# Two-layer hybrid decoder: sums of squares of the keys and the copies of two sets of transposes moved to ScalarE, three PSUM banks in turn, gating a tile later

## The chip, the cores and the metric

The program runs on one core of a Trainium2 chip. A core has TensorE (matrix multiplication, written PE in the profile, its weight loads PEld), VectorE (DVE), ScalarE (ACT), GpSimd (POOL) and SyncE (SP, which issues most DMAs). Each engine runs its own instruction stream in order and waits on semaphores for the others. The metric is the device time of one execution in microseconds (us); less is better.

## The reference

Two layers, each a mixer and a feed-forward part, for 512 new tokens (the prompt) and 8 tokens of a decode batch that share the weights. The mixer has one input projection whose columns go to a gated DeltaNet (group A, 4 heads of 128) and to a retention (group B, 4 heads of 128). What the change touches:

```python
qkv = silu(causal_conv(p_qkv, conv_w))                 # group A: q, k, v
qa, ka = l2norm(heads(q)), l2norm(heads(k))            # x * rsqrt(sum(x*x) + 1e-6), per token and head
a_low  = strict_lower((k*beta) @ k^T * decay)          # per chunk and head
u      = solve(I + a_low, v * beta)                    # v rows scaled by beta, one number per token and head
...
o_b = retention(rope(q_b), rope(k_b), v_b)             # group B
o_b = o_b * rsqrt(mean(o_b*o_b) + EPS) * ret_norm_w * silu(gate_b)
out = concat([o_a, o_b]) @ w_out
```

## The kernel before

Activations are kept transposed (features on the 128 partitions, tokens along the free axis). A weight tile of the input projection is 1024 x 128; the loop counter `t` runs over its 32 tiles of a layer: 0 to 11 retention q, k and v; 12 to 15 keys of group A; 16 to 19 the retention's gate (`gatesB`); 20 to 23 values of group A; 24 to 27 queries of group A; 28 to 31 gate of group A. Every matrix product is made of three fp32r passes: each weight tile (a slab) comes by DMA into `stage` (SP), ScalarE rounds it to `Wh` (line 1064), VectorE makes the rest `Wl` (line 1435), and `mm6` multiplies Xh·Wh, Xl·Wh, Xh·Wl for two halves of 260 columns. A tile has 8 steps of 6 such matmuls (`proj(1)` is one step, line 626). The result lies in one of two pairs of PSUM banks (0 to 3), so tile t can start only when VectorE has read tile t-2 (`tile_free0/1`).

Between the steps of the projection TensorE does the smaller work of both mixers, in an order that is written out by hand (lines 817 to 960), in banks 4 to 7. All four engines have such hand-written streams: what a `if t == 17:` holds is issued after tile 17's own work of that engine. The pieces of the change:

- `stats(i, c)`, line 718: sums of squares of a key or query head for one of 4 chunks of 128 tokens, as a matmul of the squares `sqb` with a column of ones. ScalarE makes the squares at the end of `silu_tile` (line 1180). Keys have i = 0 to 3, queries 4 to 7; each takes 4 matmuls. The keys' are put between the steps of tiles 15, 16 and 17.
- `k_rows(c)`, line 706: transposes of the keys of chunk c into PSUM; `k_copy(c)`, line 1182: ScalarE copies them to `ktok`.
- `prep(c)`, line 729: the decay exponents of chunk c (bank 5) and k·k^T (bank 6). ScalarE turns the first into `PT` by Exp with the log of the keys' root as bias (`decays`, line 1186), VectorE masks it and multiplies (`masked`, line 1555, gives `MT` and `mt_ready`), TensorE transposes (`blocks_T`), VectorE scales (`blocks_scaled`, gives `Ab` and `a_ready`). `Ab` goes by DMA to DRAM and back for a solve by VectorE (`solve`, tiles 21 to 23).
- `ret_normed(c)`, line 1612: VectorE scales the retention's rows `oR` by their roots.
- `ret_out(c)`, line 755: TensorE transposes these rows into bank 5 or 6, after tile 24, half of 25, 25, and half of 26. `gate_ret(c)`, line 1580: VectorE multiplies bank, norm weight and `gatesB`.
- `v_rows(c)`, line 694, and `v_scaled(c)`, line 1543: the value rows, transposed by TensorE, scaled by beta into `bv` by VectorE.
- `left(i)` and `right(i)`, lines 766 and 780: TensorE's steps of a block inverse that follow, beginning in tile 28.

## Time and profile before

| what | value |
|---|---|
| median of 3 runs | 1521.31 us (1519.15 to 1521.94) |
| profiled execution | 1518.86 us, its span 1517.1 us |
| PE busy | 1480.3 us, 98% of the span |
| DVE, ACT, POOL busy | 844.0, 507.2, 104.5 us |
| chain that ended last | PE 86%, DVE 8%, ACT 2%, DMA 2% |
| granted TensorE clock | 0.998 |

The span goes from the first to the last instruction of the profiled execution; the run's own time is 1.8 us more. A fp32 matmul of the program shows as two rows of instructions, a fp32r one as one row. Layer 0 lasts from 0 to about 750 us of the span, layer 1 from there; what is read in one layer at time x is found in the other at about x + 747.

### The profile page before, as it was taken

To read this page: it belongs to the slowest core of one execution; us is meant where nothing else is said; L and a number is where in the kernel's file an instruction comes from. 1 tells how busy PE (TensorE), PEld (TensorE's weight loads), DVE (VectorE), ACT (ScalarE), POOL (GpSimd) and SP (SyncE) were. 2 spreads that over 40 slices of the span, in tenths; PEclk is the share of its full clock that TensorE was granted. 3 is DMA by queue.
4 is the path that set the end of the run, shared out by engine and by line. 5 is a ranking of instruction groups with operands and counts; after the bars stand their busy time and mean duration, and the time that the engine had idled before them with its cause. 6 is when DMAs were issued, how large, how long until landed. Compare 5 with 4: busy or idle time off the path is not lost.

```text
span 1517.1 us, 28272 instructions
## 1 busy us (share of the span) xinstructions
PE 1480.3 (98%) x12164; PEld 1463.0 (96%) x12164; DVE 844.0 (56%) x1438; ACT 507.2 (33%) x919; POOL 104.5 (7%) x145
## 2 busy tenths in 40 slices
PE   7999999999999999999999999999999999999996
PEld 6999999999999999999989999999999999999996
DVE  3745685478555554423396457845785555543235
ACT  4124432435422222222241344424363222222221
POOL 0000012210000000000000001121000000000000
PEclk9999999999999999999999999999999999999999
DMA  4232133022233434222213222321223334332221
GB/s 163 98 112 84 56 102 102 29 70 76 98 126 128 144 127 145 88 95 95 73 62 106 98 84 63 101 71 39 76 71 119 132 130 142 128 116 89 93 98 57
DMA packets 57403, 147.38 MB, mean 97 GB/s; under 512 B 19008, under 2 KB 22464, under 8 KB 57280
## 3 DMA queue, kind: packets, MB, share of 16 engines
q1 hardware_dynamic: 49456, 119.88, 24.2%
q0 software_dynamic: 7824, 25.70, 4.8%
q8 instruction: 96, 1.57, 0.4%
q14 instruction: 27, 0.22, 0.1%
HBM read 132.77 MB, written 12.78 MB: 96 GB/s over the span
## 4 chain that ended last, share of the span: by engine, by line
PE 86%; DVE 8%; ACT 2%; DMA 2%; issue 1%; SPq 1%; DVEq 0%; ACTq 0%
PE PS L525 69%; PE PS L531 5%; DVE Wl L1435 2%; PE PS L544 2%; DMA stage<-w_slabs 1%; PE PS L690 1%; DVE upd L1469 1%; DVE hT L1470 1%; DVE conv L1537 1%; ACT Wh L1064 1%; PE PS L777 1%; PE PS L792 1%; PE PS L794 1%; PE PS L725 1%; DVE Xl L1452 1%
## 5 line engine op out<-in xcount | busy, mean ns | idle before, releaser
L525 PE MATMUL PS<-Xh,Wh 128*128 128x260 f32 x2464 | 514.4, 290 | 13.4 <-DVE Wl L1435 11.1
L525 PE MATMUL PS<-Xh,Wl 128*128 128x260 f32 x2464 | 496.8, 283 | 0.0
L525 PE MATMUL PS<-Xl,Wh 128*128 128x260 f32 x2464 | 496.2, 283 | 0.0
L1064 ACT ACTIVATE Wh<-stage 128x1024 fp32r<-128x1024 f32 x212 | 224.6, 1060 | 725.3 <-PE PS L525 711.8
L525 PEld LDWEIGHTS PS<-Xh,Wh 128*128 128x128 f32 x2464 | 382.9, 189 | 17.2 <-DVE Wl L1435 11.5
L525 PEld LDWEIGHTS PS<-Xl,Wh 128*128 128x128 f32 x2464 | 381.2, 189 | 0.0
L525 PEld LDWEIGHTS PS<-Xh,Wl 128*128 128x128 f32 x2464 | 380.2, 189 | 0.0
L1435 DVE TENSOR_TENSOR Wl<-stage,Wh 128x1024 fp32r<-128x1024 f32 x212 | 259.2, 1223 | 191.6 <-ACT Wh L1064 191.3
L525 PE MATMUL PS<-actH,Wh 128*128 128x260 f32 x616 | 124.4, 283 | 0.0
L525 PE MATMUL PS<-actH,Wl 128*128 128x260 f32 x616 | 123.9, 282 | 0.0
L525 PE MATMUL PS<-actL,Wh 128*128 128x260 f32 x616 | 123.8, 282 | 0.0
L1920 DVE TENSOR_TENSOR up<-PS,rb 128x520 f32<-128x520 f32 x44 | 30.8, 699 | 142.3 <-PE PS L525 142.3
L525 PEld LDWEIGHTS PS<-actL,Wh 128*128 128x128 f32 x616 | 95.1, 188 | 0.0
L525 PEld LDWEIGHTS PS<-actH,Wh 128*128 128x128 f32 x616 | 94.8, 188 | 0.0
L525 PEld LDWEIGHTS PS<-actH,Wl 128*128 128x128 f32 x616 | 94.8, 188 | 0.0
L531 PE MATMUL PS<-Xh,Wh 128*128 128x260 f32 x224 | 74.0, 330 | 0.5 <-DVE Wl L1435 0.4
L1909 DVE TENSOR_TENSOR gp<-PS,rb 128x520 f32<-128x520 f32 x44 | 30.8, 699 | 63.9 <-PE PS L525 58.3
L531 PE MATMUL PS<-Xl,Wh 128*128 128x260 f32 x224 | 63.3, 283 | 0.0
L531 PE MATMUL PS<-Xh,Wl 128*128 128x260 f32 x224 | 63.3, 282 | 0.0
L1537 DVE SCALAR_TENSOR_TENSOR conv<-raw,prm,conv 128x544 f32<-128x544 f32 x72 | 57.1, 793 | 2.4 <-ACT conv L1164 0.5
L435 POOL DMA_DIRECT2D dst<-state_ret x32 | 17.3, 542 | 457.4 <-DVE rcs L1500 294.9
L531 PEld LDWEIGHTS PS<-Xh,Wh 128*128 128x128 f32 x224 | 42.3, 189 | 2.7 <-DVE Wl L1435 0.6
(287 smaller groups left out, 1718.3 us busy)
## 6 DMA issues: line engine op xcount, KB each, us to landing
stage<-w_slabs SPq DMA_DIRECT2D x212, 512.0 KB, 3.3
dst<-state_ret POOLq DMA_DIRECT2D x32, 256.0 KB, 3.0
dst<-state_gdn POOLq DMA_DIRECT2D x32, 256.0 KB, 3.0
out_gdn_sample<-dst POOLq DMA_DIRECT2D x16, 256.0 KB, 2.8
out_ret_sample<-dst POOLq DMA_DIRECT2D x16, 256.0 KB, 3.2
hT<-x_t SPq DMA_DIRECT2D x4, 520.0 KB, 6.8
out_y_t<-hT SPq DMA_DIRECT2D x2, 520.0 KB, 3.0
out_y_t<-hT SPq DMA_DIRECT2D x2, 390.0 KB, 2.6
```

Source lines behind the costliest of these rows:

```text
L435: pool.dma_start(dst[:, u % 2], src).then_inc(s[f"dst{u % 2}_loaded"], 16)
L525: ins = mm(PS[:, 2 * slot + a, 0:HC], w[:, ws, pos, :], x[:, a, :], start=first and w is Wh and x is xh, stop=last and w is Wl)
L531: ins = mm(PS[:, 2 * slot + a, 0:HC], w[:, ws, pos, :], x[:, a, :], start=first and w is Wh and x is xh, stop=last and w is Wl)
L544: mm(PS[:, 4 + a, 0:HC], ones, sqh[:, k % 2, a, :], start=k == 0, stop=k == KT - 1).then_inc(s["x_sums"], 1)
L690: ins = mm(PS[:, 7, at_:at_ + 2], dst[:, u % 2, i, :], qkvD[:, h:2 * H + h + 1:2 * H, b], start=True, stop=True)
L725: ins = mm(PS[:, 7, at_:at_ + 1], sqb[:, i % 2, c * P:(c + 1) * P], ones[:, 0:1], start=True, stop=True)
L777: ins = mm(PS[:, 4, j * P:(j + 1) * P], T[:, i % 2, j, :], firsts(2 * (i % 2) + j // 2, b, j % 2), start=True, stop=True)
L1064: A(Wh[:, G % NW], stage[:, G % NS], ACT.Copy).then_inc(s["hi_split"], 1)
L1435: V.tensor_tensor(Wl[:, G % NW], stage[:, G % NS], Wh[:, G % NW].bitcast(fp32), ALU.subtract).then_inc(s["lo_split"], 1)
L1537: ins = V.scalar_tensor_tensor(conv[:, u], raw[:, u, w:w + CONV_N], prm[:, l, row + w * QKV:row + w * QKV + 1], conv[:, u], ALU.mult, ALU.add)
L1909: freed(V.tensor_tensor(gp[:], pj(3 if j == 1 else 0), rb[:], ALU.mult), t)
L1920: freed(V.tensor_tensor(up[:], pj(1), rb[:], ALU.mult), t + 1)
```

## The change

- The keys' 16 `stats` matmuls of a layer are gone, with the 4 squares that fed them. ScalarE instead takes the sums from the transposed rows `ktok`: 16 activations (Square, with the sum of a row as second output), 3 of 4 chunks before tile 17's weight rounding, the last after it. The root is then one Ln, one scale by -0.5, and one Exp, the Exp behind `decays(0)`.
- Without the stats between them, TensorE reaches `k_rows(0..2)` half a tile earlier in the program (middle of tile 17), `k_rows(3)` too; `prep(0)` stays at the middle of tile 18.
- On VectorE in tile 17 `masked(0)` and `decay_sums(2)` come ahead of the small products with the keys' root. The normalising of the retention rows (4 `ret_normed`) moves from tile 17 to the end of tile 19.
- The retention's transposes use banks 5, 6, 4, 5. ScalarE copies each out of PSUM with the norm weight as scale into `bv`, which is free then (`ret_out_rows`); `gate_ret` becomes a product of two SBUF tiles and comes a tile later. TensorE's next user of a bank waits for the copy (`rO_ready`) in place of the gating (`catR_done`).
- The value rows use banks 6, 4, 5, 6, and ScalarE scales them into `bv`, 4 activations a chunk (`v_scaled`), in place of one VectorE product.
- Waits of `left(0)` and `right(0)` are split to match.

TensorE, end of tile 17's steps and the keys' transposes, before (L525 is a projection step, L725 stats, L715 k_rows):

```order
L525 MATMUL PS<-Xh,Wl 128x260 x2
L725 MATMUL PS<-cf,sqb 128x1
L525 MATMUL PS<-Xh,Wh 128x260 x2
L525 MATMUL PS<-Xl,Wh 128x260 x2
L525 MATMUL PS<-Xh,Wl 128x260 x2
L725 MATMUL PS<-cf,sqb 128x1
L715 MATMUL PS<-cf,kT 128x128 [waits oR_ready,rs_ready,silu_done]
L715 MATMUL PS<-cf,kT 128x128 x11
L525 MATMUL PS<-Xh,Wh 128x260 [waits tile_free0,lo_split]
```

and now, at the middle of tile 17 (L526 is the projection step, L714 k_rows):

```order
L526 MATMUL PS<-Xh,Wh 128x260 x2
L526 MATMUL PS<-Xl,Wh 128x260 x2
L526 MATMUL PS<-Xh,Wl 128x260 x2
L714 MATMUL PS<-cf,kT 128x128 [waits oR_ready,rs_ready,silu_done]
L714 MATMUL PS<-cf,kT 128x128 x11
L526 MATMUL PS<-Xh,Wh 128x260 x2
```

The one-column matmuls are gone, and the transposes are followed by the rest of tile 17 (no wait for a free pair of banks there) where they were followed by tile 18.

ScalarE, from the last key tile to the first decays, before (L1180 squares, L1064 weight rounding, L1184 k_copy, L1189 decays):

```order
L1174 ACTIVATE qkvD<-conv 128x8
L1180 ACTIVATE sqb<-kT 128x512 [waits st_mm,silu_done]
L1064 ACTIVATE Wh<-stage 128x1024 [waits tile_done,slab0_loaded]
L1054 ACT_TABLE_LOAD
L1238 ACTIVATE nrR<-nrR 128x16 [waits nrR_pre]
L1239 ACTIVATE nrR<-nrR 128x16 [waits act_step]
L1242 ACTIVATE lrq<-PS 128x4x4 [waits st_mm]
L1243 ACTIVATE rq<-lrq 128x4x4 [waits act_step]
L1244 ACTIVATE lrq<-lrq 128x4x4 [waits act_step]
L1184 ACTIVATE ktok<-PS 128x512 [waits k_T] x4
L1189 ACTIVATE PT<-PS,lrq 128x128 [waits dec_mm,kst_ready]
L1189 ACTIVATE PT<-PS,lrq 128x128 x3
```

and now (L1188 the sums, L1061 weight rounding, L1181 k_copy, L1194 decays; ahead of these rows stand the table load, three k_copy and the sums of two chunks):

```order
L1188 ACTIVATE sqb,lrq<-ktok 128x128 [waits kt_ready]
L1188 ACTIVATE sqb,lrq<-ktok 128x128 x3
L1181 ACTIVATE ktok<-PS 128x512 [waits k_T]
L1061 ACTIVATE Wh<-stage 128x1024 [waits tile_done,slab0_loaded]
L1188 ACTIVATE dump,lrq<-ktok 128x128 [waits kt_ready]
L1188 ACTIVATE dump,lrq<-ktok 128x128 x3
L1261 ACTIVATE lrq<-lrq 128x4x4 [waits ksq_ready]
L1262 ACTIVATE lrq<-lrq 128x4x4 [waits act_step]
L1194 ACTIVATE PT<-PS,lrq 128x128 [waits dec_mm,act_step]
L1194 ACTIVATE PT<-PS,lrq 128x128 x3
L1264 ACTIVATE rq<-lrq 128x4x4
L1266 ACTIVATE nrR<-nrR 128x16 [waits nrR_pre]
```

The table load and the copies have moved ahead of the weight rounding, the sums stand on both sides of it, and the retention's root has moved behind the first decays.

VectorE, tiles 24 and 25, before (L1529 to L1531 read a tile, L1435 weight rest, L1537 convolution, L1585 gate_ret):

```order
L1531 COPY raw<-histT 128x8x3
L1435 TENSOR_TENSOR Wl<-stage,Wh 128x1024 [waits hi_split,raw_ready]
L1585 SCALAR_TENSOR_TENSOR gatesB<-PS,prm,gatesB 128x4x128 [waits tO_T,gB_ready]
L1537 SCALAR_TENSOR_TENSOR conv<-raw,prm,conv 128x544 [waits tap_ready]
L1537 SCALAR_TENSOR_TENSOR conv<-raw,prm,conv 128x544 [waits dve_step] x2
L1529 TENSOR_TENSOR raw<-PS,rb 128x512 [waits silu_done,tile_done]
L1530 TENSOR_TENSOR raw<-PS,rb 128x8
```

and now the same place of tile 25 (L1555 to L1557, L1461, L1563 and L1607 are the same functions; tile 24 has no gating at all):

```order
L1557 COPY raw<-histT 128x8x3
L1461 TENSOR_TENSOR Wl<-stage,Wh 128x1024 [waits hi_split,raw_ready]
L1563 SCALAR_TENSOR_TENSOR conv<-raw,prm,conv 128x544 [waits tap_ready]
L1563 SCALAR_TENSOR_TENSOR conv<-raw,prm,conv 128x544 [waits dve_step] x2
L1607 TENSOR_TENSOR gatesB<-bv,gatesB 128x4x128 [waits rO_ready,gB_ready]
L1555 TENSOR_TENSOR raw<-PS,rb 128x512 [waits silu_done,tile_done]
```

The first gating has moved from the middle of tile 24 to the end of tile 25 and no longer reads PSUM.

The core of the diff:

```diff
+        B_R = (5, 6, 4, 5)
-        B_V = (4, 5, 6, 4)
+        B_V = (6, 4, 5, 6)
...
@@ TensorE: v_rows, ret_out
                     if c == 0:
                         pe.wait_ge(s["silu_done"], l * QKV + 2 * H)
-                        pe.wait_ge(s["a_ready"], (l + 1) * NC)
-                    elif c < 3:
-                        pe.wait_ge(s["catR_done"], l * NC + c + 2)
+                    if c < 3:
+                        pe.wait_ge(s["rO_ready"], l * NC + c + 2)
                     else:
                         pe.wait_ge(s["bv_ready"], l * NC + 1)
...
                     pe.wait_ge(s["onR_ready"], l * NC + c + 1)
-                    if c < 2:
+                    if c == 0:
                         pe.wait_ge(s["dk_ready"], (l + 1) * NC)
+                    elif c == 1:
                         pe.wait_ge(s["mt_ready"], (l + 1) * NC)
-                    else:
-                        pe.wait_ge(s["catR_done"], l * NC + c - 1)
+                    elif c == 2:
+                        pe.wait_ge(s["a_ready"], (l + 1) * NC)
+                    else:
+                        pe.wait_ge(s["rO_ready"], l * NC + 1)
                     for h in range(H):
-                        ins = tr(PS[:, 5 + c % 2, h * P:(h + 1) * P], oR[:, c, h, :], ident)
+                        ins = tr(PS[:, B_R[c], h * P:(h + 1) * P], oR[:, c, h, :], ident)
@@ TensorE: left(0), right(0)
-                        pe.wait_ge(s["bv_ready"], (l + 1) * NC)
+                        pe.wait_ge(s["bv_ready"], l * NC + 2)
...
+                    else:
+                        pe.wait_ge(s["bv_ready"], (l + 1) * NC)
@@ TensorE: the order of tiles 15 to 18
-                        if c >= 3:
-                            stats(c - 3, b)
...
-                for i in range(1, 4):
-                    if i == 3:
-                        proj(KT // 2)
-                    for b in range(KT // 2):
-                        proj(1)
-                        if i == 1:
-                            dec_read(7, b)
-                        stats(i, b)
+                for b in range(KT // 2):
+                    proj(1)
+                    dec_read(7, b)
+                proj(KT)
                 for c in range(3):
                     k_rows(c)
                 proj(KT // 2)
                 k_rows(3)
+                proj(KT // 2)
                 prep(0)
@@ ScalarE: new functions
+                def k_sums(c):
+                    to = (dump[:], *(sqb[:, a, 0:SEQ].rearrange("p (h n) -> p h n", h=H) for a in range(2)), dump[:])[c]
+                    act.wait_ge(s["kt_ready"], l * NC + c + 1)
+                    for h in range(H):
+                        ins = A(to[:, h, :], ktok[:, c, h, :], ACT.Square, accum_out=lrq[:, c, H + h:H + h + 1])
+                    ins.then_inc(s["ksq_ready"], 1)
...
+                def ret_out_rows(c):
+                    act.wait_ge(s["tO_T"], l * NC + c + 1)
+                    A(bv[:, c], bank4(B_R[c]), ACT.Copy, scale=prm[:, l, R_RN:R_RN + 1]).then_inc(s["rO_ready"], 1)
+
+                def v_scaled(c):
+                    act.wait_ge(s["v_T"], l * NC + c + 1)
+                    act.wait_ge(s["catR_done"], l * NC + c + 1)
+                    for h in range(H):
+                        ins = A(bv[:, c, h], PS[:, B_V[c], h * P:(h + 1) * P], ACT.Copy, scale=beta[:, c, h:h + 1])
+                    ins.then_inc(s["bv_ready"], 1)
@@ ScalarE: tiles 24 to 27
+                    if t in (24, 25):
+                        ret_out_rows(2 * (t - 24))
                     if 20 <= t < 28:
                         first_tap(t - 16)
                     if 21 <= t < 29:
                         silu_tile(t - 17)
+                    if t in (24, 25):
+                        ret_out_rows(2 * (t - 24) + 1)
+                    if t in (26, 27):
+                        v_scaled(2 * (t - 26))
+                        v_scaled(2 * (t - 26) + 1)
@@ VectorE: gate_ret and its places
-                    dve.wait_ge(s["tO_T"], l * NC + c + 1)
+                    dve.wait_ge(s["rO_ready"], l * NC + c + 1)
-                    V.scalar_tensor_tensor(gatesB[:, :, a, cols], bank4(5 + c % 2), prm[:, l, R_RN:R_RN + 1], gatesB[:, :, a, cols], ALU.mult, ALU.mult).then_inc(s["catR_done"], 1)
+                    V.tensor_tensor(gatesB[:, :, a, cols], bv[:, c], gatesB[:, :, a, cols], ALU.mult).then_inc(s["catR_done"], 1)
...
-                            for c in {24: (0,), 25: (1,), 26: (3,)}.get(t, ()):
+                            for c in {26: (1,), 27: (3,)}.get(t, ()):
                                 gate_ret(c)
-                            for c in {26: (0,), 27: (2, 3)}.get(t, ()):
-                                v_scaled(c)
...
                     if t == 19:
                         blocks_scaled(1)
                         masked(3)
+                        dve.wait_ge(s["nrR_ready"], l + 1)
+                        step(V.tensor_tensor(nrR[:, 1], nrR[:, 1], cf[:, C_GQ:C_GQ + NC * H], ALU.mult))
                         blocks_scaled(2)
+                        for c in range(NC):
+                            ret_normed(c)
...
                     if t == 25:
+                        gate_ret(0)
+                    if t == 26:
                         gate_ret(2)
-                    if t == 26:
-                        v_scaled(1)
```

## Rows read from the trace of the kernel before

**Rows 1.** The page, part 1: busy us, share, instructions of each engine.
```profile
PE 1480.3 (98%) x12164; PEld 1463.0 (96%) x12164; DVE 844.0 (56%) x1438; ACT 507.2 (33%) x919; POOL 104.5 (7%) x145
```

**Rows 2.** Waits of TensorE, whole span: us in total, times, longest.
```profile
PE PS L763 <- DVE gatesB L1585: 4.9, 4, 1.5
...
PE PS L739 <- ACT ktok L1184: 0.6, 2, 0.3
```

**Rows 3.** Timeline of TensorE, tiles 16 and 17: start, us, instruction.
```profile
143.59 0.36 PE L725 MATMUL PS<-cf,sqb 128*128 128x1 f32 x2
143.81 0.49 PE L525 MATMUL PS<-Xh,Wh 128*128 128x260 f32 x2
...
147.31 0.49 PE L525 MATMUL PS<-Xh,Wh 128*128 128x260 f32 x2
...
148.25 0.49 PE L525 MATMUL PS<-Xh,Wh 128*128 128x260 f32 x2
...
151.87 0.40 PE L525 MATMUL PS<-Xh,Wh 128*128 128x260 f32 x2
...
152.59 0.40 PE L525 MATMUL PS<-Xh,Wh 128*128 128x260 f32 x2
```

**Rows 4.** Groups by line and shape, TensorE: busy us, mean ns, idle before.
```profile
L725 PE MATMUL PS<-cf,sqb 128*128 128x1 f32 x128 | 19.1, 218 | 0.0
```

**Rows 5.** Timeline of TensorE at prep(0) and prep(1).
```profile
162.83 1.13 PE L739 MATMUL PS<-cf,T 128*128 128x128 f32 x8 [0.31 <-ACT ktok L1184]
...
167.59 1.05 PE L739 MATMUL PS<-cf,T 128*128 128x128 f32 x8
```

**Rows 6.** Timeline of TensorE at the third and fourth retention transposes.
```profile
215.70 0.40 PE L525 MATMUL PS<-Xh,Wl 128*128 128x260 f32 x2
217.38 0.63 PE L763 MATMUL PS<-cf,oR 128*128 128x128 f32 x4 [1.28 <-DVE gatesB L1585]
...
222.39 0.63 PE L763 MATMUL PS<-cf,oR 128*128 128x128 f32 x4 [1.51 <-DVE gatesB L1585]
```

**Rows 7.** Timeline of VectorE, tiles 17 to 24.
```profile
160.90 2.50 DVE L1613 TENSOR_TENSOR oR<-oR,nrR 128x512 f32<-128x512 f32 x4
...
166.04 0.68 DVE L1560 TENSOR_TENSOR MT<-PS,PT 128x512 f32<-128x512 f32 x1
...
186.01 0.69 DVE L1529 TENSOR_TENSOR raw<-PS,rb 128x512 f32<-128x512 f32 x1 [2.20 <-PE PS L525]
...
214.47 0.68 DVE L1529 TENSOR_TENSOR raw<-PS,rb 128x512 f32<-128x512 f32 x1
```

**Rows 8.** Busy time by window, x instructions, clock, DMA share, GB/s.
```profile
198.20:226.30 28.10, 25.32 (x212) 24.95 (x212) 25.56 (x62) 10.48 (x21) 3.22 (x3) 1.00 0.33 99
```

**Rows 9.** Timeline of ScalarE, tiles 12, 16 and 17.
```profile
108.49 0.19 ACT L1156 ACTIVATION_READ_ACCUMULATOR dump<-oR 128x1 f32 x1
...
108.58 0.29 ACT L1156 ACTIVATE dump<-oR 128x128 f32<-128x128 f32 x1
...
108.87 0.29 ACT L1156 ACTIVATE dump<-oR 128x128 f32<-128x128 f32 x1
...
153.03 0.63 ACT L1180 ACTIVATE sqb<-kT 128x512 f32<-128x512 f32 x1
...
158.90 1.28 ACT L1054 ACT_TABLE_LOAD   x1
160.20 0.22 ACT L1238 ACTIVATE nrR<-nrR 128x16 f32<-128x16 f32 x1
...
161.14 2.04 ACT L1184 ACTIVATE ktok<-PS 128x512 f32<-128x512 f32 x4
164.06 1.14 ACT L1189 ACTIVATE PT<-PS,lrq 128x128 f32<-128x128 f32 x4 [0.89 <-PE PS L739]
```

**Rows 10.** Timeline of SyncE's queue, then of TensorE, at the block inverse.
```profile
222.06 8.21 SPq L408 DMA_DIRECT2D XX<-x_tmp  x16
...
241.38 1.14 PE L777 MATMUL PS<-XX,T 128*128 128x128 f32 x8
```

More of the change, by code:

```diff
@@ L887, in _ @@
                         if i in (1, 3, 5, 7):
-                            stats(H + i // 2, b)
+                            stats(i // 2, b)
                             dec_read(7 + i, b)
@@ L1234, in _ @@
                         silu_tile(3)
-                    if t == 17:
-                        exp_tables()
+                        exp_tables()
+                        for c in range(3):
+                            k_copy(c)
+                        for c in range(3):
+                            k_sums(c)
+                        k_copy(3)
+                    if t == 17:
+                        k_sums(3)
+                        act.wait_ge(s["ksq_ready"], (l + 1) * NC)
+                        step(A(lrq[:, :, H:2 * H], lrq[:, :, H:2 * H], ACT.Ln, bias=L2_EPS))
+                        step(A(lrq[:, :, H:2 * H], lrq[:, :, H:2 * H], ACT.Copy, scale=-0.5))
+                        decays(0)
+                        A(rq[:, :, H:2 * H], lrq[:, :, H:2 * H], ACT.Exp).then_inc(s["kst_ready"], 1)
                         act.wait_ge(s["nrR_pre"], l + 1)
@@ L1676, in _ @@
                     if t == 17:
-                        dve.wait_ge(s["nrR_ready"], l + 1)
-                        step(V.tensor_tensor(nrR[:, 1], nrR[:, 1], cf[:, C_GQ:C_GQ + NC * H], ALU.mult))
-                        for c in range(NC):
-                            ret_normed(c)
+                        masked(0)
+                        decay_sums(2)
                         dve.wait_ge(s["kst_ready"], l + 1)
@@ L1687, in _ @@
                             step.go(V.scalar_tensor_tensor(brkm[:, k], brk[:, :, 2:4], cf[:, C_MS + k:C_MS + k + 1], cf[:, C_MF + k:C_MF + k + 1].unsqueeze(2).to_broadcast([P, NC, 2]), ALU.mult, ALU.add))
-                        masked(0)
-                        decay_sums(2)
                     if t == 18:
```

33 lines of the change are left out of this document (9 added, 24 removed).

## The prediction, made before the changed kernel had run

> **What bounds the kernel.** I read the page first: TensorE is busy for 1480.3 of 1517.1 us [rows 1], so time can only be saved where TensorE has fewer instructions, or where it stands still. Then TensorE's waits: of the places that the change touches, two appear. Its line 763, the retention's transposes, waits 4 times for the gating on VectorE, 4.9 us in all, and line 739, the decay exponents, twice for a copy of keys by ScalarE, 0.6 us in all [rows 2]. Third, TensorE's timeline, for what a small matmul costs between projection steps [rows 3], and last the timelines of VectorE and ScalarE, for how early each delivers what TensorE needs. ScalarE and VectorE work beside TensorE; what they save or spend counts only where it opens or closes a wait there.
>
> **Term 1: the keys' stats matmuls.** A projection step of six matmuls takes 152.59 - 151.87 = 0.72 us alone and 148.25 - 147.31 = 0.94 with one stats matmul behind it, so 0.22. Where a decode read stands in the step already, the stats matmul takes 143.81 - 143.59 = 0.22 too [rows 3]. The group of line 725 has 128 rows, none of them behind an idle time [rows 4]; a matmul is two rows, so 64 matmuls, half of them the queries', which stay. 32 x 0.22 = 7.0 us. Nothing hides them: they stand in TensorE's own stream. (The group's mean of 218 ns is one pipelined row; two of those would be twice what the start times show.)
>
> **Term 2: stops at the retention's transposes.** The third transpose of a layer waits for bank 5, the fourth for bank 6, each until VectorE has gated the one before. Idle is 1.28 and 1.51 us in layer 0 [rows 6]. By start times a stop costs more: rows of two matmuls follow each other by 0.72 / 3 = 0.24, so the transpose at 217.38 could have started at 215.70 + 0.24 = 215.94; it lost 1.44, 0.16 over the idle figure. For 4 stops 4.9 + 0.64 = 5.5 us. After the change the third uses bank 4, whose last reader was done in tile 20; the fourth waits for ScalarE's copy of the first, made more than half a tile before. The first value rows wait for the copy of the second, 1.5 tiles wide of it.
>
> What is late next there? VectorE, which is busy for 25.56 of 28.10 us from tile 21 to tile 26 [rows 8]. Tile 26 needs the bank pair that VectorE frees by reading tile 24, at 214.47 + 0.68 = 215.2 [rows 7]. Without its stop TensorE would ask at 215.94 + 4 transposes, 0.4, = 216.3: 1.1 us to spare. This stretch of VectorE starts with DMA and solve that hang on tile 20, so it moves forward with TensorE. From there on VectorE has less to do: no gating in tile 24, none of the four v products in 26 and 27.
>
> **Term 3: the stop at prep(0)**, 0.31 us idle a layer [rows 5], by the same count 0.47: 0.9 us in both. It waits for the third key copy. The copies now come half a tile earlier against prep(0), so it goes, if ScalarE gets there.
>
> **Is ScalarE in time?** This is the new chain, and I lay it out against the start of prep(0) as zero. Transposes of the keys start 8 steps (5.8) and 16 transposes at 0.11 each (1.8) before, at -7.6; tile 16 ends 4 steps ahead of that, at -10.5. ScalarE then rounds a weight slab and does the last key tile, which took until 153.03 with tile 16's end at 151.87 - 0.72 = 151.1 [rows 3, 9], so to -8.6; the keys' rows need only this, at -7.6: 1 us to spare. Table load 1.28, to -7.3. Three copies, 2.04 / 4 = 0.51 each, bound by the transposes: to -5.5. Twelve sums: the pair of activation and accumulator read repeats every 108.87 - 108.58 = 0.29, so 3.5: to -2.0. Fourth copy -1.5, weight slab 1.06: -0.4, four sums 1.2: +0.8, Ln and scale 0.5: +1.3. Before, decays(0) began 164.06 - 162.83 = 1.2 behind prep(0) [rows 5, 9]; now 1.3 to 1.4. VectorE's product MT ended at 166.04 + 0.68 = 166.7, 3.9 behind; now about 4.1 (masked(0) has moved ahead of the small products). prep(1) asks for it at 167.59 - 162.83 = 4.8. To spare: 0.7 us. I take no new wait.
>
> The unknown in it is the sums' price. The squares of a whole head took 0.63 for 512 columns, 0.16 for 128: with that the chain ends 2 us earlier, and gains nothing, for decays(0) then waits for prep(0). Were activation (0.29) and accumulator read (0.19) not overlapped, 0.48 a pair, the chain would be 16 x 0.19 = 3.0 later, less the 0.7: 2.3 a layer lost, 4.6 in all [rows 9]. I take 0.29, for it is the same instruction with the same shape in tiles 12 to 15.
>
> Here a rule of the Trainium skill speaks against the change. First the row: the table load took 1.28 us, 158.90 to 160.18, and the next activation began at 160.20 [rows 9], so nothing follows the load. The skill (ScalarE: Activation LUTs, What ACT_TABLE_LOAD costs) counts a drain of about 1.38 us besides, 2.66 in all, for each switch. By the row the load, now ahead of the key copies, ends as they may begin, and costs nothing; by the page it would push the copies back by some 1.2 us. The trace does not agree with the page here, unless the drain lay ahead of the load, where ScalarE had just ended an activation at 158.89.
>
> **The rest costs nothing, and this is why.** Four ret_normed, 2.50 us, now stand ahead of tile 20's first read, where VectorE had been idle for 2.20 [rows 7]: 0.3 late, and that read was followed by a wait for the weight rounding anyway. If that cover were gone, it is 0.3 a layer. Gating as a product of two SBUF tiles: 2.50 / 4 = 0.62, not above what it was. ScalarE's four copies of 512 columns, between the key copy's 0.51 and the square's 0.63 each [rows 9], I take 0.6; its 16 scaled v activations as four decays, 1.14 a chunk [rows 9], bounded below by 0.51 for a chunk. That is 7.0 us over tiles 24 to 27, while ScalarE was busy for only 10.48 of 28.10 us [rows 8]. Behind them on ScalarE are weight roundings (each needed three tiles later) and the block inverse's first copies, needed by right(0) half a tile behind left(0). The wait that GpSimd has for all four transposes ends 3 us earlier with them. SyncE's 16 loads for left(0) are issued by 230.3, left(0) was at 241.38 [rows 10]; TensorE now comes 3.2 closer, and 8 stay.
>
> **Sum.** 7.0 + 5.5 + 0.9 = 13.4 us. The profiled execution took 1518.86 (span 1517.1 and 1.8 around it), so 1505.5; it is 2.4 below the median of the runs, 1521.31, and against that it gives 1507.9.
>
> **Rivals.**
> - *A new wait at prep(1).* The 0.7 us in ScalarE's chain is not there: an accumulator read that hides less, a semaphore wait between sets of sums. For it: some 20 ScalarE instructions in a row from the first key copy to the decays. Against it: the rows above. The price is up to 4.6 us; at half of it 1510.2. The skill's drain (same page and section) would be a case of it.
> Worked out from rows alone, a load that ends 1.2 us later gives 0.5 a layer: 1508.9.
> - *The stop only moves.* VectorE is near its limit in tiles 21 to 25, and TensorE, having lost its stops at 763, waits for the next bank pair. It needs VectorE to be 1.1 + 3.1 = 4.2 us later against TensorE than now to eat all of term 2; for: 25.56 of 28.10; against: only 0.3 us is added ahead of it and work is taken out. All of it: 1521.3 - 7.9 = 1513.4.
> - *Slower.* The keys' sums stand in the serial path from tile 16 to MT; TensorE's prep(1) stands in order ahead of all else. To lose 13.4 us this must be 6.7 + 0.7 = 7.4 us late a layer, which it is from 0.29 + 7.4 / 16 = 0.75 us a sum. At 0.85 a layer loses 8.3: 1521.3 - 13.4 + 16.6 = 1524.5. Only a pair 2.6 times as long as in tile 12 does this.
> - *It doesn't do what it says*: if the stops were really due to a semaphore other than the gating (GpSimd's, or a DMA's), only term 1 remains: 1514.3. The transposes' only other wait, for ret_normed, ended 40 us before in the old order, so this is small.
>
> **Chances.** Forecast, 1506 to 1509.4: 0.70. Wait at prep(1): 0.13. Stop only moves: 0.10. Other semaphore: 0.04. Slower: 0.03. The predicted time is the forecast's, 1507.9. The three shown runs lie within 2.8 us of each other, so the medians add some 1 us either way. Range 1505.2 to 1512.8: it leaves out the slower case, half of the moved stop, and most of term 1 alone. A change of under 0.2% (3 us) this measurement can't tell from none: same 0.02, slower 0.03, faster 0.95.
>
> **What the profile after would show.** Line 725 has 64 rows in place of 128, and steps of tile 16's second half and tile 17 follow at 0.72: term 1. Line 763 has no entry in TensorE's waits: term 2; if instead the projection's first matmul of tile 25, 26 or 27 waits for VectorE's read, the stop has moved. Line 739 on a wait for the key copy gone: term 3; on a wait for MT with 4 entries or 2: the chain on ScalarE is late, and decays(0) starts more than 2 us behind prep(0). Accumulating squares at a pitch over 0.3 us, or idle time behind the table load, would show why. Right(0) waiting for v copies would show ScalarE overfull in tile 27. I am wrong if the saving is under 11 us or over 16.

## The result, and the profile after

| | before | after |
|---|---|---|
| median of the runs | 1519.96 us (5 runs, 1519.15 to 1521.94) | 1505.94 us (5 runs, 1504.80 to 1511.83) |
| profiled execution, its span | 1518.86, 1517.1 us | 1505.94, 1504.2 us |
| granted TensorE clock, mean | 0.998 | 0.997 |

The ratio is 0.9912 (95% interval 0.9898 to 0.9926): 14.0 us less by the medians, 12.9 by the spans. 1507.9 was predicted, with 13.4 us as the sum of three terms. The sum was taken off a median of 1521.31 for the kernel before; with two more runs that median is 1519.96. So of the 1.96 us by which the time came out lower, 1.35 are the base, and 0.6 the saving.

TensorE first. The page's first part, with the columns of [rows 1]:

```profile
PE 1472.4 (98%) x12100; PEld 1456.0 (97%) x12100; DVE 842.2 (56%) x1430; ACT 524.2 (35%) x1015; POOL 106.2 (7%) x145
```

64 rows fewer, 7.9 us less busy; ScalarE took 17 us more, off the path. The groups of the two lines in question, with the columns of [rows 4]:

```profile
L722 PE MATMUL PS<-cf,sqb 128*128 128x1 f32 x64 | 8.9, 208 | 0.0
L763 PE MATMUL PS<-cf,oR 128*128 128x128 f32 x32 | 4.8, 272 | 0.0
```

The stats (line 722 now) are down from 128 rows to 64, and no retention transpose has idle time before it. TensorE's waits, which answer to [rows 2]; lines 763 and 736 (739 before) are gone from them, and one of these entries is new:

```profile
PE PS L526 <- DVE Xl L1771: 1.3, 2, 0.6
PE PS L690 <- DMA dst<-state_gdn: 0.7, 2, 0.4
PE PS L526 <- DVE mT L1813: 0.6, 2, 0.3
```

The new one is in the middle: the decode reads of tile 28 wait for their state, which they didn't before. TensorE's timeline at the places of [rows 5, 6, 10], start, us, instruction:

```profile
158.74 1.05 PE L736 MATMUL PS<-cf,T 128*128 128x128 f32 x8
159.62 1.06 PE L739 MATMUL PS<-kT 128*128 128x128 f32 x8
163.41 1.05 PE L736 MATMUL PS<-cf,T 128*128 128x128 f32 x8
...
211.76 0.60 PE L763 MATMUL PS<-cf,oR 128*128 128x128 f32 x4
...
215.07 0.60 PE L763 MATMUL PS<-cf,oR 128*128 128x128 f32 x4
...
230.06 0.38 PE L690 MATMUL PS<-qkvD,dst 128*128 128x2 f32 x2 [0.28 <-DMA dst<-state_gdn]
...
234.47 1.14 PE L777 MATMUL PS<-XX,T 128*128 128x128 f32 x8
```

The last retention transpose is at 215.07 where it was at 222.39, 7.3 us earlier; left(0) is at 234.47 where it was at 241.38, 6.9 earlier: 0.4 was given back at line 690. ScalarE's chain, which answers to [rows 9]:

```profile
150.43 1.28 ACT L1051 ACT_TABLE_LOAD   x1
151.86 1.58 ACT L1181 ACTIVATE ktok<-PS 128x512 f32<-128x512 f32 x3
153.30 0.32 ACT L1188 ACTIVATE dump<-ktok 128x128 f32<-128x128 f32 x1
...
153.59 0.32 ACT L1188 ACTIVATE dump<-ktok 128x128 f32<-128x128 f32 x1
...
160.05 1.14 ACT L1194 ACTIVATE PT<-PS,lrq 128x128 f32<-128x128 f32 x4
```

A sum takes 153.59 - 153.30 = 0.29 us, and decays(0) begins 160.05 - 158.74 = 1.31 behind prep(0). VectorE, which answers to [rows 7]:

```profile
162.03 0.68 DVE L1582 TENSOR_TENSOR MT<-PS,PT 128x512 f32<-128x512 f32 x1
...
179.62 3.03 DVE L1635 TENSOR_TENSOR oR<-oR,nrR 128x512 f32<-128x512 f32 x4
```

MT is ready at 162.71, 0.70 ahead of prep(1) at 163.41.

Last, the two queues at the block inverse. SyncE's (XX<-x_tmp are the small x loads of the inverse, stage<-w_slabs the weight slabs), which answers to [rows 10]:

```profile
217.36 8.27 SPq L409 DMA_DIRECT2D XX<-x_tmp  x16
225.68 5.45 SPq L368 DMA_DIRECT2D stage<-w_slabs  x2
```

and GpSimd's, which issues the state loads:

```profile
224.97 1.12 POOL L436 DMA_DIRECT2D dst<-state_gdn  x2 [4.68 <-PE PS L690]
```

The two state loads now stand against the end of the 16 small x loads and a weight slab of 512 KB, issued 0.7 us behind them. By the view of the tile `dst` from 220 to 240 us, four such loads:

```profile
DMA to landing us min/median/max: 2.9/3.1/4.5
```

The slower one of the two took 4.5 us, and 4.6 in layer 1. Before, GpSimd issued them at 232.32, 10.3 us behind the first x load in place of 7.6, and 2 us behind the slab; they took 2.9 to 3.2. The state loads follow TensorE, which came 7.3 us forward; the x loads follow VectorE's solve, which came 4.7 forward.

### The profile page after: what moved, and what is told of

The parts are those of the page before. It is cut to its first block, busy times and chain, and to the rows that moved or that the text cites. A ratio compares the mean times of both kernels' runs of the same rounds, so it can differ in the third digit from the quotient of the medians.

```text
span 1504.2 us, 28232 instructions
## 1 busy us (share of the span) xinstructions
PE 1472.4 (98%) x12100; PEld 1456.0 (97%) x12100; DVE 842.2 (56%) x1430; ACT 524.2 (35%) x1015; POOL 106.2 (7%) x145
## 4 chain that ended last, share of the span: by engine, by line
PE 91%; DVE 5%; DMA 2%; ACT 1%; issue 1%; POOL 0%; SPq 0%; DVEq 0%; ACTq 0%
PE PS L526 73%; PE PS L532 5%; PE PS L545 2%; DMA stage<-w_slabs 1%; DVE Wl L1461 1%; PE PS L690 1%; DVE upd L1495 1%; DVE hT L1496 1%; PE PS L777 1%; PE PS L794 1%; PE PS L796 1%; DMA dst<-state_gdn 1%; DVE Xl L1478 1%; PE PS L993 0%; ACT Wh L1061 0%
## 5 line engine op out<-in xcount | busy, mean ns | idle before, releaser
L526 PE MATMUL PS<-Xh,Wh 128*128 128x260 f32 x2464 | 513.1, 289 | 13.2 <-DVE Wl L1461 10.9
L526 PE MATMUL PS<-Xh,Wl 128*128 128x260 f32 x2464 | 496.7, 283 | 0.0
L526 PE MATMUL PS<-Xl,Wh 128*128 128x260 f32 x2464 | 495.9, 283 | 0.0
L1061 ACT ACTIVATE Wh<-stage 128x1024 fp32r<-128x1024 f32 x212 | 224.5, 1060 | 693.2 <-PE PS L526 680.9
L526 PEld LDWEIGHTS PS<-Xh,Wh 128*128 128x128 f32 x2464 | 382.8, 189 | 17.0 <-DVE Wl L1461 11.3
L526 PEld LDWEIGHTS PS<-Xl,Wh 128*128 128x128 f32 x2464 | 381.2, 189 | 0.0
L526 PEld LDWEIGHTS PS<-Xh,Wl 128*128 128x128 f32 x2464 | 380.1, 189 | 0.0
L1461 DVE TENSOR_TENSOR Wl<-stage,Wh 128x1024 fp32r<-128x1024 f32 x212 | 259.3, 1223 | 193.3 <-ACT Wh L1061 192.8
L526 PE MATMUL PS<-actH,Wh 128*128 128x260 f32 x616 | 124.3, 283 | 0.0
L526 PE MATMUL PS<-actH,Wl 128*128 128x260 f32 x616 | 123.8, 282 | 0.0
L526 PE MATMUL PS<-actL,Wh 128*128 128x260 f32 x616 | 123.7, 282 | 0.0
L526 PEld LDWEIGHTS PS<-actL,Wh 128*128 128x128 f32 x616 | 95.1, 188 | 0.0
L526 PEld LDWEIGHTS PS<-actH,Wh 128*128 128x128 f32 x616 | 94.8, 188 | 0.0
L526 PEld LDWEIGHTS PS<-actH,Wl 128*128 128x128 f32 x616 | 94.8, 188 | 0.0
L1563 DVE SCALAR_TENSOR_TENSOR conv<-raw,prm,conv 128x544 f32<-128x544 f32 x72 | 60.4, 839 | 2.4 <-ACT conv L1161 0.5
```

The costliest lines, as they stand in the source:

```text
L526: ins = mm(PS[:, 2 * slot + a, 0:HC], w[:, ws, pos, :], x[:, a, :], start=first and w is Wh and x is xh, stop=last and w is Wl)
L1061: A(Wh[:, G % NW], stage[:, G % NS], ACT.Copy).then_inc(s["hi_split"], 1)
L1461: V.tensor_tensor(Wl[:, G % NW], stage[:, G % NS], Wh[:, G % NW].bitcast(fp32), ALU.subtract).then_inc(s["lo_split"], 1)
L1563: ins = V.scalar_tensor_tensor(conv[:, u], raw[:, u, w:w + CONV_N], prm[:, l, row + w * QKV:row + w * QKV + 1], conv[:, u], ALU.mult, ALU.add)
```

## The experiments

Twelve runs: nine edits, two of them run twice (2 and 12, 9 and 11), and the changed kernel itself once more (10); "the median before" is that of the kernel before on the same chip, 1520.44 for 1 to 4, 1520.82 for 5 to 8, 1521.33 for 9 and 10, 1521.16 for 11 and 12. The edits are cut to a few lines.

**1. The keys' part alone.**

```diff
 # the kernel before, with k_sums, the stats of the keys taken out,
 # the new order of TensorE's tiles 15 to 18 and of VectorE's tiles 17 to 19
+                        for c in range(3):
+                            k_copy(c)
+                        for c in range(3):
+                            k_sums(c)
```

> The kernel before with the keys' part alone: no stats matmuls for keys, sums on ScalarE, order of tiles 16 to 19 as in the changed kernel; transposes of the retention and gating as before. Theory (savings add up; each is in TensorE's stream): the keys' matmuls and the stop at prep(0), 4.18 us a layer by the two traces (163.80 against 159.62 us for the same matmul), so 8.4 us less than before; the four stops at the retention's transposes stay at 1.3 to 1.5 us each. Rival (one cause is hidden behind the other: TensorE comes earlier and waits longer at the retention's transposes, since VectorE is near its limit there): under 5 us less, with stops at the transposes that have grown by the difference.

Measured: 1513.37 us, ratio 0.9953 (0.9941 to 0.9965), 7.1 us less where 8.4 was expected; by the spans 6.9. From the retention's first preparatory transposes (110.49) to prep(0)'s second half (160.47) it takes 49.98 us, exactly what the full change takes (109.64 to 159.62), against 54.03 before (109.77 to 163.80): 4.05 a layer, 8.1 for both. Of the rest, 0.7 us lie outside the edit: this execution came that much later to the first place. The stops at the retention, which stay, took 5.3 us in all where they took 4.9:

```profile
PE PS L760 <- DVE gatesB L1587: 5.3, 4, 1.5
```

Three of them are as they were; the third transpose of layer 1 stopped for 1.01 us in place of 0.62. That is the rival's mechanism, at a small part of its size.

**2. The retention's and values' part alone**, run twice (the second time as 12).

```diff
 # the kernel before, with ret_out_rows and v_scaled on ScalarE, B_R, B_V, gate_ret a tile later
-                        pe.wait_ge(s["catR_done"], l * NC + c - 1)
+                        pe.wait_ge(s["rO_ready"], l * NC + 1)
```

> The kernel before with the retention and v part alone: banks 5, 6, 4, 5, copies and v scaling on ScalarE, gating a tile later; the keys' stats matmuls stay. Theory: the four stops go, 5.6 to 6.2 us, and a new stop of about 0.4 us a layer appears at the decode reads after the third transposes of v (TensorE comes earlier against the loads of the state), so 4.8 to 5.5 us less than before. Rival (the gain needs the keys' part to have VectorE ready): under 3 us.

Measured: 1516.56, ratio 0.9979 (0.9967 to 0.9990), and 1515.97, ratio 0.9968 (0.9959 to 0.9978), with 12 runs each from 1513.2 to 1521.4. The profiled execution, one of the fastest, has a span of 1511.4, 5.7 less, and no wait of the transposes; the new stop of 0.4 us a layer that was expected isn't in it. The medians are 3.9 and 5.2 us below the median before, where 4.8 to 5.5 was expected: the term is there in a good run, and a median loses up to 2 us of it to something that comes and goes (see 12). 6.9 + 5.7 = 12.6 by the spans, where both parts together gave 12.9: they add up.

**3. Two banks in place of three**, the copies by ScalarE kept.

```diff
-        B_R = (5, 6, 4, 5)
-        B_V = (6, 4, 5, 6)
+        B_R = (5, 6, 5, 6)
+        B_V = (4, 5, 6, 4)
```

> The changed kernel with two PSUM banks in turn for the retention's transposes (5, 6, 5, 6) as before the change, v rows in 4, 5, 6, 4; ScalarE still copies. Theory (the early copy on ScalarE ends the stops, not the third bank): in the changed kernel's trace the first copy ends at 207.3 and the third transpose is at 211.8, the second at 213.4 and the fourth at 215.1, so no stop, and the time of the changed kernel within 0.5 us (12.9 us less than before). Rival (the third bank is what frees TensorE): two stops a layer are back, of 1 us or more each, 8 to 10 us less than before.

Measured: 1506.93, ratio 0.9914 (0.9901 to 0.9928), 13.5 us less where 12.9 was expected, with no wait at the transposes. The third bank isn't what took the stops away. (A stop of 0.2 us at left(0), which waits here for the last value rows, is new.)

**4. Three banks alone**, gating and v products left on VectorE.

```diff
 # the kernel before
+        B_R = (5, 6, 4, 5)
-        B_V = (4, 5, 6, 4)
+        B_V = (6, 4, 5, 6)
```

> The kernel before with the banks 5, 6, 4, 5 and v rows in 6, 4, 5, 6, all else as before: VectorE still gates straight from PSUM in tiles 24 to 26. Theory (banks alone do little): the third and fourth transposes no longer stop, but the first v rows, right behind the fourth, need bank 6, which VectorE gates at 222.2 us where TensorE would come at 219.6: one stop of some 2.6 us a layer in place of two of 1.4 and 1.7, 0.5 to 1.5 us less than before in all. Rival (the bank is what counts): 5 to 6 us less.

Measured: 1525.65, ratio 1.0036 (1.0024 to 1.0049): 5 us slower. A miss; the waits show why:

```profile
PE PS L703 <- DVE gatesB L1587: 7.0, 2, 4.9
```

The stops have left the transposes and stand at the first value rows, which need bank 6 back: 7.0 us where there were 4.9. In layer 0 the stop is 4.88 us, in layer 1 2.17, where 2.6 was expected for each. In VectorE's timeline the gating that frees the bank comes behind the read of a tile and the weight rest that follows it; GpSimd's rows of the same time stand below:

```profile
222.82 1.39 DVE L1533 COPY raw<-histT 128x24 f32<-128x24 f32 x1
224.24 2.13 DVE L1437 TENSOR_TENSOR Wl<-stage,Wh 128x1024 fp32r<-128x1024 f32 x1
226.30 0.74 DVE L1587 SCALAR_TENSOR_TENSOR gatesB<-PS,prm,gatesB 128x512 f32<-128x512 f32 x1
```

```profile
222.37 1.80 POOL L490 MEMSET XX<- 128x2048 f32 x1 [22.78 <-PE PS L765]
224.14 3.25 POOL L464 TENSOR_TENSOR T<-MT,mask 128x512 f32<-128x512 f32 x2
```

The small copy took 1.39 us in place of 0.17, and ended as GpSimd's memset did; the weight rest took 2.13 in place of 1.23, beside GpSimd's products. Together that is 2.1 us. In layer 1, where both ran at their usual length, the gating ended 2.7 us behind the start of the read, and not 4.8. So layer 1 shows the price of the order alone, and it is near the expected one; the rest of layer 0's stop goes with two VectorE instructions that ran long beside GpSimd. No run holds GpSimd back, so this is read from one place and not shown as a cause.

The rest is in the clock, as the windows around the first stop show (busy us with instructions of PE, PEld, DVE, ACT and POOL, then granted clock, DMA share, GB/s):

```profile
210.00:220.00 10.00, 10.00 (x87) 10.00 (x86) 9.48 (x25) 4.45 (x10) 0.00 (x0) 1.00 0.17 52
220.00:230.00 10.00, 5.12 (x33) 4.92 (x32) 9.82 (x12) 2.59 (x6) 5.02 (x3) 0.75 0.51 139
230.00:240.00 10.00, 10.00 (x82) 10.00 (x81) 6.48 (x11) 3.08 (x6) 1.12 (x2) 0.91 0.35 73
```

Behind the stop of 4.9 us the granted clock is below 1.00, and back at it by 240: 10 us times what is missing to 1.00 gives at most 3.4 us here (for part of it TensorE still stood), and a window at 0.83 behind the second stop another 1.7. A further window at 0.83, from 20 to 30 us, is far ahead of the edit.

**5. The sums twice**: each set of four activations doubled.

```diff
                     for h in range(H):
+                        ins = A(to[:, h, :], ktok[:, c, h, :], ACT.Square, accum_out=lrq[:, c, h:h + 1])
+                    step(ins)
+                    for h in range(H):
```

> The changed kernel with every sum of squares of the keys done twice on ScalarE (16 more activations a layer, their sums unused, and 4 short waits between). Theory (ScalarE's chain from the key copies to MT has only 0.7 us to spare at prep(1)): 16 x 0.29 + 4 x 0.05 = 4.8 us later, so TensorE stops at prep(1) for some 4.1 us a layer, 8.2 us more than the changed kernel, with the stop shown at the decay matmuls. Rival (ScalarE has room, 35% busy): less than 1 us more.

Measured: 1521.77, ratio 1.0003 (0.9995 to 1.0012): the whole gain is gone. The waits, then ScalarE's timeline:

```profile
PE PS L736 <- DVE MT L1585: 9.1, 2, 4.5
```

```profile
169.62 1.14 ACT L1197 ACTIVATE PT<-PS,lrq 128x128 f32<-128x128 f32 x4
```

prep(0) was at 163.06, so decays(0) begins 6.56 behind it where it was 1.31: 5.25 later for 16 more sums. Less the 0.70 to spare that is 4.55, and the stop is 4.54. The stops explain 9.1 of the 15 us to the changed kernel; the mean granted clock of 0.993 against 0.997 explains some 6 more (0.004 x 1521). By windows 1.7 us of that lie behind each of the two stops, and 3.4 in the window from 20 to 30 us (0.66), far ahead of the edit.

**6. The old order** of roots, masks and normalising on ScalarE and VectorE, all else as changed. (One thing is not as before: the Exp of the keys' root stays behind the first decays.)

```diff
-                        masked(0)
-                        decay_sums(2)
+                        dve.wait_ge(s["nrR_ready"], l + 1)
+                        step(V.tensor_tensor(nrR[:, 1], nrR[:, 1], cf[:, C_GQ:C_GQ + NC * H], ALU.mult))
+                        for c in range(NC):
+                            ret_normed(c)
```

> The changed kernel with the order of roots and masks of before in tile 17: retention's root first, keys' root fully before the first decays, on VectorE the four normalised retention rows and the small products ahead of masked(0). Theory: VectorE starts the normalising at 160.0, ends it at 162.7, then products 0.8, mask and MT 1.5: MT at 165.0 in place of 162.7, where prep(1) is at 163.4. A stop of 1.6 us a layer, 3 us more than the changed kernel; the reordering is needed because the sums took the time to spare. Rival (order indifferent): within 0.5 us of the changed kernel.

Measured: 1510.25, ratio 0.9929 (0.9917 to 0.9941), 10.6 us less than before where the changed kernel has 14: 3.4 more, where 3 was expected. 2.6 of it are two stops at prep(1), of 1.3 each. MT ended 5.98 behind prep(0) in place of 3.97. Without the new order the sums don't fit; whether ScalarE's part of it or VectorE's does more was not tried apart.

**7. VectorE made late** in tile 23, by four products.

```diff
+                        if t == 23:
+                            for _ in range(4):
+                                step(V.tensor_tensor(Yb[:], over_heads(m_gt), over_heads(m_le), ALU.mult))
```

> The changed kernel with four unused products of 128x512 on VectorE at the end of tile 23 (0.65 to 0.7 us each, 2.7 us), behind the solve. Theory (VectorE has 1.0 us to spare for tile 26's pair of banks): a stop of some 1.7 us a layer at the first projection matmul of tile 26 or a little less, 2.5 to 3.5 us more than the changed kernel. Rival (VectorE is not near its limit once gating and v scaling are gone from it): under 0.5 us more.

Measured: 1514.39 (1510.40 to 1519.84), ratio 0.9963 (0.9948 to 0.9978), over twice the loss expected. The stops are not much larger than expected, 4.1 us in all for 3.4:

```profile
PE PS L526 <- DVE raw L1556: 4.1, 2, 2.2
```

The span of its profile is 11.0 over the changed kernel's: 4.1 for these stops, and 6.8 for what is missing to 1.00 in the granted clock. That falls into two parts. 1.7 us lie behind layer 0's stop of 2.2 us (the window from 210 to 220 at 0.83). 5.1 us lie behind a stop of 0.39 us at the decode reads that follow, at 234.15 (0.81 and 0.67 in the two windows of 10 us from 230), which is not of this edit's making: the changed kernel has it too. Layer 1's stop of 1.9 us has no such stretch behind it.

**8. The slab among the x loads**, to keep it from the state loads.

```diff
+                            if i:
+                                slab(l * SLABS + n)
                             sp.wait_ge(s["x_zeroed"], l * 2 + i + 1)
```

> The changed kernel with SyncE's load of weight slab 31 put between the two groups of 8 block inverse loads, in place of behind them. Theory (the new stop at the decode reads, 0.28 and 0.38 us idle, comes from two state loads issued at 225.5 us together with this 512 KB slab, so that the first took 4.5 us in place of about 3): slab and state loads no longer meet, the stop is gone, 0.8 us less than the changed kernel in the span. Rival (the state load waits for its buffer, or for the 16 small loads): the stop stays, same time. Risk: the second group of block inverse loads is later, and its first user, at 234.5, could wait.

Measured: 1511.92 (1505.79 to 1517.55), ratio 0.9933 (0.9917 to 0.9948): 8.9 us less than before where the changed kernel has 14, so 5 worse and not 0.8 better. In layer 0 the slab now came 0.7 us behind the state loads, with the second half of the x loads behind it, and one state load took 5.8 us (4.9 in layer 1); TensorE stopped for 1.6 us at the decode reads in layer 0, and for 0.4 in layer 1. Behind the first the two windows from 230 have 0.78 and 0.88; behind the small one, in layer 1:

```profile
970.00:980.00 10.00, 9.42 (x78) 9.25 (x78) 8.14 (x14) 8.00 (x24) 1.11 (x2) 0.98 0.59 158
980.00:990.00 10.00, 10.00 (x48) 10.00 (x48) 1.29 (x2) 1.05 (x4) 2.23 (x3) 0.51 0.19 64
990.00:1000.00 10.00, 10.00 (x90) 10.00 (x89) 3.75 (x7) 3.05 (x7) 3.21 (x3) 1.00 0.17 57
```

From 980 to 990 TensorE is busy all the time and issues 48 matmuls, not 90, at a granted clock of 0.51, the lower of its two levels.

**9 and 10. The slab behind the state loads, beside the changed kernel itself.**

```diff
+                        if n == 31:
+                            sp.wait_ge(s["dst1_loaded"], 16 * (l * 16 + 6))
                         slab(l * SLABS + n)
```

> The changed kernel, but SyncE issues weight slab 31 only once the two state loads of tile 28 have landed. In the changed kernel those loads took up to 4.5 us to landing, with the slab issued 0.7 us behind them, against 2.9 to 3.0 before, and TensorE stood 0.3 and 0.4 us at the decode reads. Theory (the loads are slow because the slab shares the DMA engines with them, and a stop there is at times followed by a stretch in which TensorE runs at the lower clock, which makes the runs differ): landing back at about 3.0 us, no wait at the decode reads in tile 28, the profiled span 0.5 to 1 us shorter, and the runs within 1503 to 1507, none with a mean clock under 0.996. The slab, about 4 us later at 229.7, still lands 5 us ahead of its rounding at 238.6. Rival 1 (the loads are slow for another reason, the 16 small loads of XX ahead of them): they stay at 4.5 us and nothing changes. Rival 2 (the stretches at the lower clock have nothing to do with the stop): the stop goes, and some runs still take 5 to 7 us more, with a mean clock of 0.994 or less.

> The changed kernel unaltered, on the same chip and against the same runs of the kernel before, as the measure for the run beside it. All theories: median 1504.5 to 1507.5, ratio 0.991 +- 0.002. If the lower clock behind a short stop is a matter of chance from run to run, one or two of the runs are 5 to 8 us longer, with a mean clock of 0.994 or less; if the 1511.8 us seen once was something of its own, none is.

Measured: 1506.93 (4 runs, to 1507.72), ratio 0.9905 (0.9890 to 0.9919), and 1507.12 (4 runs, to 1510.84), ratio 0.9902 (0.9886 to 0.9919). In 9 the state loads landed after at most 3.7 us and the stop was gone, but its span of 1504.7 isn't shorter than the first 1504.2: it has a window at 0.83 from 20 to 30 us, 1.7 us, which the other has not. The profiled execution of 10 is the one of 1510.84, so the same kernel is to be seen with its loss. Its timeline in layer 1:

```profile
970.75 0.38 PE L690 MATMUL PS<-qkvD,dst 128*128 128x2 f32 x2 [0.55 <-DMA dst<-state_gdn]
971.00 0.49 PE L526 MATMUL PS<-Xh,Wh 128*128 128x260 f32 x2
971.33 0.40 PE L526 MATMUL PS<-Xl,Wh 128*128 128x260 f32 x2
...
973.13 0.64 PE L526 MATMUL PS<-Xh,Wl 128*128 128x260 f32 x2
...
982.17 0.64 PE L526 MATMUL PS<-Xl,Wh 128*128 128x260 f32 x2
...
983.24 0.40 PE L526 MATMUL PS<-Xl,Wh 128*128 128x260 f32 x2
...
983.72 0.61 PE L794 MATMUL PS<-T,S 128*128 128x128 f32 x4
```

The same row goes from 0.40 to 0.64 us and back. From the read at 970.75 to line 794 it is 12.97 us; in the first profile of this kernel, with a stop of 0.38 at the same place and no slow stretch, it was 978.91 - 970.64 = 8.27:

```profile
970.64 0.38 PE L690 MATMUL PS<-qkvD,dst 128*128 128x2 f32 x2 [0.38 <-DMA dst<-state_gdn]
...
978.91 0.61 PE L794 MATMUL PS<-T,S 128*128 128x128 f32 x4
```

The stretch behind a stop of half a microsecond cost 4.7 us more.

**11 and 12. The kernels of 9 and 2 again.**

> The kernel of e9_slab_after_states once more, unaltered, for more runs of it: 4 of 4 stayed at 1505.4 to 1507.7, where the changed kernel had 2 of 9 at 1510.8 and 1511.8. Theory (without the stop at the decode reads there is no stretch at the lower clock behind it): no run above 1508.5, mean clocks 0.996 or more, no entry of the decode reads in TensorE's waits. Rival (four runs were luck): at two in nine, one or two of five runs at 1510 or more, with 0.994 or less.

> The kernel of e2_retention_only once more, unaltered. Its 12 runs reached from 1513.2 to 1521.4, with mean clocks of 0.997 to 0.993, and the one profile was of the fastest. Theory (a stop of some tenths at the decode reads, in runs in which the state loads land late, and a stretch at the lower clock behind it): the runs spread again by 4 us or more, and if the profiled run is above 1515, its trace has such a stretch between 220 and 260 or 960 and 1000 us, behind a wait for dst. Rival (the stretches lie behind other stops, as the one of 0.3 us at prep(0), or at the start): the trace of a longer run has them there.

11: 1506.37 (4 runs), ratio 0.9903 (0.9889 to 0.9918); but the profiled one is 1510.29, so the expectation that none would be above 1508.5 failed. Its timeline has the stop again:

```profile
230.23 0.38 PE L692 MATMUL PS<-qkvD,dst 128*128 128x2 f32 x2 [0.55 <-DMA dst<-state_gdn]
```

and its windows the stretch behind it, at 0.60 and 0.89:

```profile
230.00:240.00 10.00, 9.77 (x52) 9.77 (x53) 4.70 (x6) 4.71 (x15) 0.94 (x1) 0.60 0.30 107
240.00:250.00 10.00, 10.00 (x81) 10.00 (x79) 3.75 (x7) 3.05 (x7) 3.37 (x4) 0.89 0.33 107
```

The slab had been held back to 230.20. What was in the way this time were the x loads, as SyncE's and GpSimd's queues show:

```profile
220.19 8.20 SPq L409 DMA_DIRECT2D XX<-x_tmp  x16
```

```profile
224.87 1.12 POOL L438 DMA_DIRECT2D dst<-state_gdn  x2 [4.13 <-PE PS L692]
```

The x loads began 6.5 us behind the second of the two stores that they follow, in place of 4.0; why is open. The state loads came 4.7 us behind the first x load, and one took 4.7 us. In 9, 7.6 and 7.8 us behind it with no slab near, they took at most 3.7; in the changed kernel, at 7.6 with the slab, 4.5 and 4.6. So the slab and the x loads each make the state loads late, and holding back the slab cures only one of them. Over the 8 runs of that kernel and 9 of the changed one the medians are 1506.6 and 1507.0, with one and two runs above 1510: no difference that this can tell. Behind a stop at the decode reads the clock fell in five profiles (7, 8, 10, 11, 12), and in all 14 it never fell in mid-kernel without a stop ahead of it. But stops there of 0.28 and 0.38 us (the first profile), 0.32 (3), 0.74 (5) and 0.88 (6) had no fall behind them: a late load is not enough. That a version without them would be faster is not shown.

12 was profiled in a run of 1518.7, with stops at the decode reads of 1.0 us in all, the longest 0.78 at 234.07, and a clock of 0.78 and 0.71 in the two windows of 10 us from 230, as expected. The clocks of all 24 runs fit this: 0.997 or 0.998 in those up to 1514.7, 0.993 in those from 1520.7. So the spread of 2 is the clock's; that it falls at the decode reads is shown by one profile.

## Why the prediction was right

**Term 1 and term 3** (7.0 + 0.9 = 7.9): 8.1 measured, by the same stretch of program in both kernels, and again in experiment 1. The price of 0.22 us for a stats matmul between steps holds.

**Term 2** (5.5): in layer 0 the last transpose moved 7.32 against 4.18 for prep(0), 3.14 for two stops (1.44 + 1.67 predicted). In layer 1 the two stops are smaller,

```profile
963.95 0.63 PE L763 MATMUL PS<-cf,oR 128*128 128x128 f32 x4 [0.62 <-DVE gatesB L1585]
968.97 0.63 PE L763 MATMUL PS<-cf,oR 128*128 128x128 f32 x4 [1.51 <-DVE gatesB L1585]
```

and give 2.5 (the last is at 955.56 now, 13.41 earlier, and prep(0) 10.92 earlier). The bank was not needed. By experiments 3 and 4 it is the part that ScalarE took over, the copy out of PSUM, in place of the gating by VectorE that came late. The copy and the later gating came together in every run, so what each does alone is open. The prediction put the third transpose's freedom down to bank 4; that step was beside the point.

**The chain on ScalarE.** Sums at 0.29, decays(0) at 1.31 (1.3 to 1.4 predicted), MT at 3.97 (4.1), 0.70 to spare (0.7). Experiment 5 put 5.25 us more into it and the stop was what was left over the spare. Nothing followed the table load: it ended at 151.71, and the next activation began at 151.86. The 0.7 us to spare at prep(1) are all there. The drain of 1.38 us that the Trainium skill (ScalarE: Activation LUTs, What ACT_TABLE_LOAD costs) counts for a switch is not to be seen behind the load here either.

**What was missed.** "Of the loads, 8 stay" looked at left(0), which is the last to use them, and not at the queue they share. The state loads of tile 28 go with TensorE, and TensorE came nearer to the x loads than VectorE allowed. The step that failed is "the rest costs nothing": the new stops took 0.7 us idle in the profiled run, and 0.9 by start times (7.32 - 6.91 in layer 0, 13.41 - 12.91 in layer 1). 8.1 + 5.6 - 0.9 = 12.8, and the spans differ by 12.9; neither profile has a low clock ahead of its last 20 us, so these two can be compared. The medians differ by 14.0 and, in the repeat, by 14.2; the 1 us between is within what the runs of one kernel differ by. So the 13.4 came as near as it did with some luck: the stops that it left out, and the clock that can fall behind them (4.7 us in one run of the repeat, a third of the gain), are of that size. The median of 1505.94 lies just under the forecast's 1506 to 1509.4 and within the range, for the base's sake. ret_normed took 3.03 and not 2.5 us at its new place, hidden all the same.

**The rivals.** The wait at prep(1) was 0.7 us away, and experiments 5 and 6 reached it. The stop that only moves is what experiment 4 made, at another place than the rival's. There the four stops of 4.9 us became two of 7.0, and the clock took the rest. The 1.1 us to spare at tile 26's banks held: in the profile after, VectorE's read ends at 210.42 + 0.60 = 211.02 and TensorE has issued its transposes at 211.76 + 0.36 = 212.12. In experiment 7 the four products took 2.9 us and the stops were 2.15 and 1.94, so there it was 0.8 to 1.0. The rival of another semaphore gives 1514.3, which leaves out term 3; with it, it would be 1513.4.

## What to carry to other kernels

Two things free a PSUM bank: another bank, or a reader with time. Look at which engine frees it before adding one; another bank alone moved the stops to a later place, and the kernel was 5 us slower, 2 of it in the stops and most of the rest in the clock behind them. And after a cut on the bound engine, see which of the loads move with it and which don't: here the ones that kept their distance from each other did no harm, and the others met in the queues. A stop there of half a microsecond cost ten times that when the clock fell behind it. A profile of one execution may not show this: compare the granted clock of several runs before a small difference is put down to an edit.

## What the runs showed of the hardware

- TensorE's clock fell to its lower level in some executions and not in others. At the decode reads of tile 28 it fell for about 10 us (5.1 us are missing to 1.00) behind stops of 0.39 (experiment 7), 0.44 (8), 0.55 (10 and 11) and 0.78 us (12), and for about 7 us behind 1.61 (8); not behind 0.16 (10), 0.24 (12), 0.28 and 0.38 (after), 0.32 (3), 0.74 (5) and 0.88 (6). What decides it there was not found. At other places it fell, with 1.7 us missing each time, behind 2.15 (7), 2.17 (4) and 4.5 us (5, twice), and with up to 3.4 behind 4.9 (4); not behind 1.28 and 1.51 (before), 1.30 (6, twice) and 1.94 (7).
- The windows from 20 to 30 us, behind a stop in which TensorE waits for ScalarE and that ends at 22 to 24 us, have 1.00 in eight profiles, where that stop was 1.17 to 1.98 us; 0.83 in five (experiments 3, 4, 6, 8, 9), where it was 2.33 to 2.88; and 0.66 in one (5), where it was 4.44. 9 and 11 are one kernel, and differ in this by 1.7 us.
- The clock falls at the end of every profile too, where TensorE has no more work: in the changed kernel 0.80 in the window from 1490 to 1500. This takes part in a run's mean clock and costs nothing.
- 256 KB from a state tensor took at most 3.2 us to landing when issued 2 us behind the last slab and x load (before), 3.7 at the end of the 16 x loads of 16 KB alone (9), 4.5 and 4.6 with a 512 KB slab issued 0.7 us later as well (after), 4.7 in the midst of the x loads without a slab (11), and 5.8 with a slab and x loads behind it (8); each figure is the slower of two loads.
- An activation of 128 x 128 with an accumulated sum repeats every 0.29 us, also 12 times in a row.
- In experiment 4 a copy of 128 x 24 on VectorE took 1.39 us in place of 0.17 beside a memset on GpSimd, and a subtraction of 128 x 1024 took 2.13 in place of 1.23 beside GpSimd's products.
